# Nine blocks of the first expert product in 512 columns, their two halves added by ScalarE and VectorE

## The reference

```python
q = (hc @ wq).reshape(T, PEER_HEADS, 2, PEER_KEY_DIM)
...
g = jax.nn.softmax(sc, axis=-1)
u_g = exp_u[e]
act = jax.nn.gelu(jnp.einsum('td,thkd->thk', hc, u_g).astype(jnp.float32), approximate=False)
w = (g * act).astype(hc.dtype)
return jnp.einsum('thk,thkd->td', w, exp_v[e])
```

## Time and profile before

| | |
|---|---|
| Median of 3 runs | 969.23 us (968.88 to 969.53) |
| The profiled execution's own time | 968.99 us |
| Its span (first to last instruction) | 967.1 us |
| TensorE busy, share of the span | 946.4 us, 98% |
| VectorE busy | 728.9 us, 75% |
| ScalarE busy | 475.7 us, 49% |
| First product, blocks 0 to 127 | to 611 us |
| Second product | 611.42 us to 960.5 us |

### The profile page before, as it was taken

How to read it: one execution, slowest core, us unless ns; L and a number is a source line. 1 busy time by engine, 2 the same in 40 slices (tenths; PEclk the granted TensorE clock), 3 DMA queues, 4 the chain that set the end, 5 groups by cost and what they waited for, 6 DMA issues and landing times.

```text
span 967.1 us, 16417 instructions
## 1 busy us (share of the span) xinstructions
PE 946.4 (98%) x6366; PEld 857.4 (89%) x6366; DVE 728.9 (75%) x1406; ACT 475.7 (49%) x858; POOL 158.7 (16%) x81
## 2 busy tenths in 40 slices
PE   7999999999999999999999999999999999999997
PEld 5988798899999999999999999888888888888885
DVE  5859799759999978899999986555555555555556
ACT  4453664354444544444444444544555544445554
POOL 1000003969789800000000000000000000000000
PEclk9999999999999999999999999999999999999999
DMA  8998748046655555454554455566666666666663
GB/s 342 371 412 338 317 186 346 2 155 184 186 180 189 177 175 156 154 159 158 159 154 154 154 154 184 186 196 194 192 187 195 192 194 195 196 195 192 191 191 124
DMA packets 47903, 192.62 MB, mean 199 GB/s; under 512 B 5314, under 2 KB 7506, under 8 KB 46419
## 3 DMA queue, kind: packets, MB, share of 16 engines
q1 hardware_dynamic: 47762, 191.55, 60.3%
q0 software_dynamic: 64, 0.03, 0.0%
HBM read 190.48 MB, written 1.07 MB: 198 GB/s over the span
## 4 chain that ended last, share of the span: by engine, by line
PE 89%; DVE 5%; POOL 3%; ACT 1%; issue 1%; DMA 1%; SPq 0%; DVEq 0%; ACTq 0%
PE banks L1149 23%; PE banks L1125 13%; PE banks L1129 12%; PE banks L1126 12%; PE banks L1156 12%; PE banks L1140 3%; PE banks L847 3%; POOL wq_low L453 3%; PE banks L843 2%; PE banks L800 1%; DVE sc_w L1264 1%; PE banks L916 1%; PE banks L780 1%; PE banks L1105 1%; PE banks L816 1%
## 5 line engine op out<-in xcount | busy, mean ns | idle before, releaser
L1558 DVE TENSOR_TENSOR lo<-raw,hi 128x1024 fp32r<-128x1024 f32 x213 | 266.8, 1254 | 166.4 <-ACT hi L656 164.8
L656 ACT ACTIVATE hi<-raw 128x1024 fp32r<-128x1024 f32 x255 | 270.5, 1061 | 168.3 <-PE banks L1156 168.3
L1125 PE MATMUL banks<-h2r,hi 128*128 128x256 f32 x1024 | 256.4, 288 | 0.0
L1126 PE MATMUL banks<-h2r,hi 128*128 128x256 f32 x1024 | 251.0, 283 | 0.0
L1149 PE MATMUL banks<-hi,wsplit 128*128 128x512 f32 x992 | 245.1, 389 | 0.5 <-DVE wsplit L1651 0.5
L1149 PEld LDWEIGHTS banks<-hi,wsplit 128*128 128x128 f32 x992 | 186.1, 188 | 39.4 <-issue 0.7
L1126 PEld LDWEIGHTS banks<-h2r,hi 128*128 128x128 f32 x1024 | 196.5, 192 | 0.0
L1125 PEld LDWEIGHTS banks<-h2r,hi 128*128 128x128 f32 x1024 | 196.0, 191 | 0.0
L1129 PE MATMUL banks<-h2r,lo 128*128 128x256 f32 x1024 | 143.7, 283 | 0.2 <-POOL lo L462 0.2
L1156 PE MATMUL banks<-lo,wsplit 128*128 128x512 f32 x496 | 132.6, 389 | 0.0
L1129 PEld LDWEIGHTS banks<-h2r,lo 128*128 128x128 f32 x1024 | 132.1, 192 | 0.5 <-POOL lo L462 0.4
(11 more groups left out here) (243 smaller groups left out, 971.4 us busy)
## 6 DMA issues: line engine op xcount, KB each, us to landing
raw<-in_u_t SPq DMA_DIRECT2D x128, 512.0 KB, 3.5
raw<-in_v_b SPq DMA_DIRECT2D x128, 512.0 KB, 3.7
wq<-in_wq SPq DMA_DIRECT2D x2, 4096.0 KB, 19.9
sh_w<-in_w_mod SPq DMA_DIRECT2D x8, 512.0 KB, 13.0
sc_w<-in_w_mod SPq DMA_DIRECT2D x8, 512.0 KB, 13.4
win<-in_w_in SPq DMA_DIRECT2D x8, 512.0 KB, 14.3
win<-in_w_in SPq DMA_DIRECT2D x1, 4096.0 KB, 21.2
sc_w<-in_w_mod SPq DMA_DIRECT2D x2, 2048.0 KB, 23.5
```

The lines of the kernel that those rows point to most:

```text
L656: nc.scalar.activation(high_at(n), raw[n % RAW][:, :], ACT.Copy).then_inc(high_ready, 1)
L1125: nc.tensor.matmul(dst, w, h2r[:, 0, c, :], start=(c == 0), stop=False)
L1126: nc.tensor.matmul(dst, w, h2r[:, 1, c, :], start=False, stop=False)
L1558: nc.vector.tensor_tensor(lo_t[n % RAW][:, :], raw[n % RAW][:, :], high_at(n).bitcast(F32), ALU.subtract).then_inc(vector_low, 1)
```

## The change

For blocks 118 to 126 (`WIDE_FROM <= n < BLOCKS - 1`) the pair of 256-column matmuls of one chunk becomes one matmul of 512 columns: its moving operand is both activation parts, and its output the whole bank, left half the product with part 0 and right half that with part 1. The low part's 8 matmuls still go to the left half. ScalarE copies the right half into `u_part`, VectorE adds the left half to it into `u_sum`, and the gelu reads `u_sum` instead of the bank. Blocks 0 to 117 and block 127 stay as they were. Two semaphores are new, and to make room four others go: the `win1a` chunks 1 to 4 now count on the `win0` semaphore of the same chunk, and whoever waited for either waits for both.

```diff
+WIDE_FROM = 118
...
+        u_part = at("u_part", M0 + 2560, [P, 2, SEQ])
+        u_sum = at("u_sum", M0 + 3072, [P, 2, SEQ])
...
-        win1a_in = [sem(f"win1a_in{c}") for c in range(DC)]
+        win1a_in = [sem(f"win1a_in{c}") if c in (0, 5, 6, 7) else win0_in[c] for c in range(DC)]
...
+        part_out, summed = map(sem, ("part_out", "summed"))
...
+        def win_count(c):
+
+
+            return 16 if c in (0, 5, 6, 7) else 32
...
-                        sc.wait_ge(landed[c], 16)
+                        sc.wait_ge(landed[c], win_count(c))
...
             def gelu(n):
 
                 before = gated_before(n)
+                if WIDE_FROM <= n < BLOCKS - 1:
+                    sc.wait_ge(late_act, n - GATE_AT - 2)
+                    sc.wait_ge(summed, n - WIDE_FROM + 1)
+                    nc.scalar.activation(gelu_out[:, n % 2, :], u_sum[:, n % 2, :], ACT.Gelu).then_inc(act_out, 1)
+                    return
...
+            def copy_part(n):
+
+                sc.wait_ge(block_used, n + 1)
+                if n >= WIDE_FROM + 2:
+                    sc.wait_ge(summed, n - WIDE_FROM - 1)
+                nc.scalar.activation(u_part[:, n % 2, :], bank[4 + n % 2][:, SEQ:2 * SEQ], ACT.Copy).then_inc(part_out, 1)
...
             for n in range(1, STREAM):
+                if WIDE_FROM <= n - 1 < BLOCKS - 1:
+                    copy_part(n - 1)
                 if HI <= n + 1 < STREAM:
                     high(n + 1)
                 if n <= BLOCKS:
...
-                            pe.wait_ge((win0_in if name == "win0" else win1a_in)[c], 16)
+                            pe.wait_ge((win0_in if name == "win0" else win1a_in)[c], win_count(c))
...
+                both = bank[4 + n % 2].rearrange("p (k s) -> p k s", k=2)
                 for c in range(DC):
                     w = hi_t[:, n % HI, c * P:(c + 1) * P]
-                    nc.tensor.matmul(dst, w, h2r[:, 0, c, :], start=(c == 0), stop=False)
-                    nc.tensor.matmul(dst, w, h2r[:, 1, c, :], start=False, stop=False)
+                    if WIDE_FROM <= n < BLOCKS - 1:
+                        nc.tensor.matmul(both, w, h2r[:, :, c, :], start=(c == 0), stop=False, skip_group_check=True)
+                    else:
+                        nc.tensor.matmul(dst, w, h2r[:, 0, c, :], start=(c == 0), stop=False)
+                        nc.tensor.matmul(dst, w, h2r[:, 1, c, :], start=False, stop=False)
...
+            def add_parts(n):
+
+                ve.wait_ge(part_out, n - WIDE_FROM + 1)
+                if n >= WIDE_FROM + 2:
+                    ve.wait_ge(act_out, n - 1)
+                nc.vector.tensor_tensor(u_sum[:, n % 2, :], bank[4 + n % 2][:, 0:SEQ], u_part[:, n % 2, :], ALU.add
+                                        ).then_inc(summed, 1)
...
+                if WIDE_FROM <= n - 1 < BLOCKS - 1:
+                    add_parts(n - 1)
                 if GATE_AT < n - 1 < BLOCKS:
                     late(n - 1)
```

More of the change, by code:

```diff
@@ L1129, in u_block @@
                     last = nc.tensor.matmul(dst, lo_t[n % RAW][:, c * P:(c + 1) * P], h2r[:, 0, c, :],
-                                            start=False, stop=(c == DC - 1))
+                                            start=False, stop=(c == DC - 1), skip_group_check=(WIDE_FROM <= n < BLOCKS - 1))
                 last.then_inc(block_used, 1)
```

## The result

The changed kernel takes 978.29 us (median of 6, 976.75 to 979.2), the kernel before 969.27 us in the same series: a ratio of 1.009, 95% interval 1.008 to 1.010. It is slower, as forecast, by 9.0 us instead of 6.0, and its median lies 0.7 us above the top of the range.

The account below looks back on a forecast made before the run. TensorE bounds the kernel, but in nine blocks a loop of waits through ScalarE and VectorE, 3.27 us a round against 2.77, takes over: 968.99 + 5.98 = 974.97, with 0.24 for the median 975.2 us; range 973.4 to 977.6.

Parts of the forecast that it names:

- The ring: Blocks 118 to 126: copy, high, low, addition, gelu wait in turn, 3.27 us a round; +5.98 us in all; chance 0.78.
- addition to gelu: VectorE to ScalarE in each new block: addition 0.42 us plus a hop of 0.04, 0.46 us together.
- The handover: Before second block 0: TensorE waits about 3.3 us for wlow(0), behind high(129) and low(129); 2.6 us of the loss.
- TensorE's gain: Blocks 118 to 126: 512-column matmuls save 0.10 to 0.11 us a block, 1.0 us over nine.
- Against: End of the kernel: matmuls stop after 960.12, granted clock below 1.00 only from 965 on, counted against a clock fall.
- rival B: Pause before the second product: the ring, and TensorE's clock falls in 3.3 us; 1.8 us more, 977.0; chance 0.12.
- The price of 1.8 us: Clock fall before the second product: eight matmuls at the lower and higher clock, 3.78 - 1.99 = 1.8 us.
- perhaps once more: Clock fall before the second product: its 1.8 us might be paid a second time; that double price lay outside the range.
- The merged semaphores: win0 chunks 1 to 4 wait for win1a: ScalarE's rounding of chunk 3 starts 0.6 to 1.4 us later, cost 0.

Follow-up runs that it names:

- four-block kernel: The changed kernel with only blocks 118 to 121 in the new form, in place of nine: 971.21 us, ratio 1.0021 to the kernel before.
- all-first kernel: Changed kernel with high ahead of the copy on ScalarE, addition ahead of low and wlow(0) ahead of low(129) on VectorE: 968.22 us, ratio 0.9988 to kernel before.
- second profile: Profile from the changed kernel measured once more, unaltered, in the second series: 977.14 us, kernel before 969.7, ratio 1.0078.
- narrow kernel: The changed kernel with 256-column matmuls again in the nine blocks, copy, addition and order unchanged: 977.75 us, ratio 1.0089 to the kernel before.
- short pause: The kernel before with two linked, unneeded VectorE additions (1024 and 512 columns) ahead of wlow(0): 972.49 us, ratio 1.0026.
- pause kernels: The kernel before with two or three linked, unneeded VectorE additions ahead of wlow(0): 972.49 us with two, 976.71 us with three.
- long pause: The kernel before with three linked, unneeded VectorE additions (1024, 512 and 1024 columns) ahead of wlow(0): 976.71 us, ratio 1.0055.

## Why the prediction was right and wrong

- **The ring** was right, in its members, its order and its being the bound: 3.32 us for a round, against 3.27 forecast. The four-block kernel shows that it is paid by the block, the kernel with narrow matmuls that TensorE's own time counts for 0.4 us beside it, and the all-first kernel, with the same instructions, that the loss in the blocks comes from the order and not from the work.
- **The term mis-sized in it** is "addition to gelu 0.42 and a hop, I take 0.04". The addition took 0.42, but from its end at 590.79 to the gelu at 590.88 it is 0.09, and the gelu out of SBUF lets the copy start 0.32 us after it, in place of 0.29. The copy lets `high` start after 0.27 in place of 0.29, and `low` follows after 1.08 in place of 1.09. That is 0.05 in a round, and 0.54 over the path (6.52 for 5.98). Both were inside the bounds.
- **The handover** was right: 3.07 us of wait for `wlow`, forecast about 3.3.
- **TensorE's gain** was put at 1.0 us and is 0.8, since the eight matmuls of a new block take 1.84 us and not the 1.82 of the second product; in the changed kernel it is hidden in the waits. The Trainium skill's sentence on larger matmuls (Perfetto Trace Analysis, section Matmuls) holds for the matmuls alone, by 3%, and the kernel lost by it all the same.
- **The step that failed** is "Against" in rival B: a granted clock of 1.00 for some time after the last matmul of all was taken as a sign that it would hold in the pause. So B got 0.12, and the sum has no term for the clock. What the runs showed in its place: in both profiles of the changed kernel the clock fell, and second block 0 took 4.16 and 4.41 us, not the usual 2.81, which is 1.35 and 1.60 us. The row at the end was one case and not a rule. There the clock fell at 965.28 (worked out from the 0.57 of the stretch 965 to 967), 4.8 us after TensorE had stopped at 960.51; in the changed kernel it fell 2.5 us after TensorE had stopped at 614.50, and in the second profile 3.8 us after. The warning of TensorE: Matmul & The Clock Gate in the Trainium skill, section Why this matters for your kernels, held in these two; in the narrow kernel, with a pause of 3.14 us, it did not. The price of 1.8 us was about right, and "perhaps once more" was in no term of the sum.
- **The tail** of 0.37 us was not foreseen, and its cause is not settled.
- **The range.** 5.98 + 0.54 + 0.37 gives 6.9 us, which is 976.1; the narrow kernel's execution without a fall took 975.96. The medians are 1.0 us above that in the second series and 2.2 in the first. The clock's fall has this size, but outside the profiles that is argued and only in part. A mean clock of 0.997 goes with one fall in the profiles and 0.994 with two (the short pause), and three of the first six executions had 0.994 and took 978.35 to 979.2 us. But 978.0 and 978.22 had 0.997, as the profiled 976.75 had, and in the second series the slowest, 977.43, had 0.999. Something else adds a microsecond or two to some executions. The 2.2 us from VectorE and GpSimd in the pause kernels' profiles are a candidate, as 8 of the 27 executions of the kernel before in that series took 970.9 to 973.6 us; no profile of the changed kernel shows it, and it stays open. The range ended at 977.6, since the ring's error, the tail and the fall were never added to one another.
- **The merged semaphores** were right: 0.7 us more of wait on ScalarE, nothing on TensorE.

## What to carry to other kernels

When an operation is added on two engines that take their lists in order, write down the loop of waits that goes through both lists, and go on until no loop is longer than the bound engine's step: the new work here (some 0.3 us a block on each engine) was free in one order and cost 6.5 us up to the second product in another, and one exchange out of two left a loop of 3.06 us. A range should add the errors that can come together, and one place in a trace where the clock held is no evidence that it will hold in another. A pause of a dense TensorE is to be priced at more than its length, as a chance and not a threshold.

## What the runs showed of the hardware

- The granted clock fell to 0.50 at pauses of 3.79, 3.07 (twice), 2.80, 2.52 and 1.92 us, and did not at 3.14, 1.92, 1.14 and 0.54, nor at the 1.19 us pause near 147 us that all fourteen profiles have. It fell 0.6 and 0.2 us before the first matmul behind the pause (the first profile of the changed kernel, and the long pause) and 0.7 to 1.5 us after it in the other four. It was low for 3.4 us each time, which cost 1.35 to 1.7 us.
- A gelu of 128x256 takes 0.42 us out of SBUF and 0.38 out of PSUM, and a VectorE addition of 128x256 with one operand in PSUM 0.42, as in SBUF.
- 512-column matmuls over two pieces of memory, eight with as many weights, start 0.230 us apart (1.84 for 8), in the second product 0.227.
- Where VectorE (a 128x2048 operation) and GpSimd (a 128x1024 subtraction) began within 0.02 us of each other near 320 us, twelve profiles had 2.29 us for VectorE and 4.56 or 4.57 for GpSimd, and the two of the pause kernels had 4.54 and 2.40.
